# A seven-product matrix multiplication: moving VectorE's second-term sums ahead of a norm's bias passes, and two turned tiles further back on TensorE

## The reference, cut to what matters

```
mix = concat([att, u], -1) @ w_out            # (tokens, 1024) @ (1024, 1024)
h   = layer_norm(ALPHA * h + mix, ln1_g, ln1_b)
v   = mem @ w_cv                              # keys and values of the cross-attention,
q   = h @ w_cq                                # then its queries
```

## Time and profile before

| | us |
|---|---|
| median of three runs | 1035.78 (1035.64 to 1036.3) |
| the profiled execution | 1041.34 |
| its span, first to last instruction | 1039.6 |
| mixer's products of pairs 0 and 1, first to last | 362.21 to 421.51 |

### The profile page before, as it was taken

The page is one execution under the profiler, slowest core; times in us unless marked ns, Lnnn a source line. Parts: engine busy times, 40 slices in busy tenths (PEclk is TensorE's granted clock), DMA queues, the critical chain, the costliest instruction groups (busy, mean ns, idle before and its releaser), DMA issues.

```text
span 1039.6 us, 10109 instructions
## 1 busy us (share of the span) xinstructions
PE 914.8 (88%) x3322; PEld 472.8 (45%) x3322; DVE 524.3 (50%) x830; ACT 237.1 (23%) x582; POOL 321.1 (31%) x352
## 2 busy tenths in 40 slices
PE   4999999799989879999999999967969999999900
PEld 4555466344544434445558544553434444444300
DVE  4899999964632286746225465354311111211156
ACT  5321423234493111201004302131101111111101
POOL 6921043334453252400004403313251221112047
PEclk9999999899999999999999999977989999999955
DMA  9310301403003002220032031356997999998462
GB/s 335 135 41 0 122 0 63 100 1 82 1 1 122 1 0 81 81 82 0 1 116 88 3 160 69 154 240 223 419 404 273 420 421 418 390 416 344 182 245 121
DMA packets 46197, 165.11 MB, mean 159 GB/s; under 512 B 8640, under 2 KB 14144, under 8 KB 33856
## 3 DMA queue, kind: packets, MB, share of 16 engines
q1 hardware_dynamic: 39424, 151.85, 37.9%
q0 software_dynamic: 6720, 12.60, 3.2%
HBM read 156.88 MB, written 18.03 MB: 168 GB/s over the span
## 4 chain that ended last, share of the span: by engine, by line
PE 55%; POOL 4%; DVE 4%; issue 3%; DMA 2%; ACT 1%; POOLq 0%; DVEq 0%
PE ps L2470 8%; PE ps L2499 7%; PE ps L2301 7%; PE ps L2473 5%; PE ps L2340 5%; PE ps L2274 5%; PE ps L2238 4%; PE ps L2006 3%; PE ps L2184 2%; PE ps L2447 2%; PE ps L2109 2%; POOL hres L729 2%; PE ps L2081 1%; PE ps L2330 1%; PE ps L2018 1%
## 5 line engine op out<-in xcount | busy, mean ns | idle before, releaser
L1324 DVE SCALAR_TENSOR_TENSOR cat<-early,cpar,cat 128x798 f32<-128x798 f32 (+2 forms) x150 | 141.6, 944 | 4.9
L844 POOL TENSOR_SCALAR hT<-hT,rinv 128x512 f32<-128x512 f32 (+1 forms) x48 | 67.8, 1424 | 94.1 <-DVE rinv L1446 94.1
L2006 PE MATMUL ps<-ring,hT 128*128 128x512 f32 (+1 forms) x256 | 90.4, 513 | 0.0
L2006 PE MATMUL ps<-hT,ring 128*128 128x256 f32 (+1 forms) x256 | 86.1, 500 | 4.6 <-issue 2.9
L910 POOL DMA_INDIRECT pair_rows<-hT,sidx x22 | 22.1, 1002 | 182.8 <-DVE hT L1933 181.9
L1923 DVE COPY memx<-ps 128x256 f32<-128x256 f32 x22 | 9.3, 424 | 131.2 <-PE ps L2482 131.2
L2006 PEld LDWEIGHTS ps<-hT,ring 128*128 128x128 f32 x256 | 50.5, 199 | 38.8 <-issue 32.9
L718 POOL TENSOR_SCALAR lnt<-mv 128x1 f32<-128x1 f32 x28 | 14.2, 505 | 168.5 <-DVE mv L746 167.4
L2006 PEld LDWEIGHTS ps<-ring,hT 128*128 128x128 f32 x256 | 48.4, 191 | 38.7 <-issue 36.3
L1438 DVE TENSOR_REDUCE nmax<-ps 128x2 f32<-128x1024 f32 (+1 forms) x24 | 25.1, 1046 | 73.5 <-PE ps L2134 73.4
L851 POOL TENSOR_SCALAR memx<-memx,rinv 128x256 f32<-128x256 f32 x24 | 22.0, 924 | 129.7 <-DVE rinv L1402 129.7
(11 more groups left out here) (337 smaller groups left out, 1760.6 us busy)
## 6 DMA issues: line engine op xcount, KB each, us to landing
ring<-w_down SPq DMA_DIRECT2D x16, 1024.0 KB, 17.0
early<-w_gate SPq DMA_DIRECT2D x12, 1024.0 KB, 9.5
early<-w_up SPq DMA_DIRECT2D x12, 1024.0 KB, 13.7
ring<-w_gate SPq DMA_DIRECT2D x10, 1024.0 KB, 12.3
ring<-w_up SPq DMA_DIRECT2D x10, 1024.0 KB, 16.4
scr<-w_down SPq DMA_DIRECT2D x8, 1024.0 KB, 15.6
cat<-w_down SPq DMA_DIRECT2D x8, 1024.0 KB, 15.4
scr<-w_gate SPq DMA_DIRECT2D x5, 1024.0 KB, 9.3
```

Of the source, the lines that this page charges most:

```text
L844: g.tensor_scalar(sprob[u % 4][:, 0:width], sprob[u % 4][:, 0:width], rinv[:, u % 4:u % 4 + 1], None, ALU.mult).then_inc(prob_ready, 1)
L1324: ins = v.scalar_tensor_tensor(out=out, in0=src, scalar=cpar[:, c, k:k + 1], in1=out, op0=ALU.mult, op1=ALU.add)
L2006: last = t.matmul(out_of(bank), lhs(k), rhs(k), start=(k == 0), stop=(k == KC - 1))
```

## The change

Nothing is added or removed; eight pieces change places on two engines. `mix_term(0, "P2")` and `mix_term(1, "P2")` on VectorE stand ahead of the bias pass of tile 0 and of T4, `mix_term(0, "P6")` stands between T4 and T1, the bias pass of tile 0 behind T1, and that of tile 1 behind the sum for P7. On TensorE the turned tile 0 comes behind P5 in place of P7, and the turned tile 1 behind P3 in place of P4.

```diff
             mix_rows(0, 3)
             mix_rows(0, 4)
-            dve_bias(dve, LN_1[0], link)
+            mix_term(0, "P2")
+            mix_term(1, "P2")
             dve.wait_ge(mx_combined, 4)
             v.tensor_tensor(mxT["T4"], mxB[1][0], mxT["T2"], ALU.subtract).then_inc(mx_combined, 1)
+            mix_term(0, "P6")
             v.tensor_tensor(mxT["T1"], mxB[0][1], mxB[0][0], ALU.subtract).then_inc(mx_combined, 1)
+            dve_bias(dve, LN_1[0], link)
+            mix_term(0, "P7")
             dve_bias(dve, LN_1[1], link)
-            mix_term(0, "P2")
-            mix_term(1, "P2")
-            for term in ("P6", "P7", "P4", "P5"):
-                mix_term(0, term)
+            mix_term(0, "P4")
+            mix_term(0, "P5")
...
                 mx_term(a, "P7", mxS["S3"], mxT["T3"])
                 if a == 0:
-                    h1_T(0)
                     pe.wait_ge(mx_combined, 7)
                 mx_term(a, "P4", A22, mxT["T4"])
                 if a == 0:
-                    h1_T(1)
                     pe.wait_ge(mx_combined, 8)
                 mx_term(a, "P5", mxS["S1"], mxT["T1"])
+                if a == 0:
+                    h1_T(0)
                 pe.wait_ge(mx_combined, (6, 12)[a])
                 mx_term(a, "P3", mxS["S4"], mxB[1][1])
+                if a == 0:
+                    h1_T(1)
```

## The result

| | before | changed |
|---|---|---|
| median of the eleven runs of each that were then compared | 1039.80 (1034.91 to 1043.26) | 1031.37 (1028.32 to 1035.36) |
| ratio, 95% interval | | 0.9934 (0.9914 to 0.9953) |
| profiled execution | 1041.34 | 1032.55 |
| its span | 1039.6 | 1030.8 |

Faster, by 8.4 us between the medians; the interval of the ratio is 4.9 to 8.9 us of 1039.8. The profiled execution became 8.79 us shorter, against 8.8 forecast (1032.5); that they agree so closely is in part luck, since the parts that the change does not touch came out alike in these two profiles and differ by some us in others (the last table of the experiments). The median, 1031.37, lies above the range that the prediction gave (1025.8 to 1029.8): the kernel before, run eleven times, has its median 4 us above that of the three runs shown first.

A forecast was written before the change was run, and what follows sets the result against it. TensorE, busy 914.8 of 1039.6 us, was taken as the bound. 9.47 us of wait and slow clock, less new waits of 0.5 and 0.2, gave 8.8; 1035.78 - 8.8 = 1027.0 us, range 1025.8 to 1029.8.

The forecast's parts named there:

- P7's wait: TensorE ahead of P7 of pair 0: 6.45 us of waiting for the bank of P2 would go.
- The slow clock: TensorE during P7 of pair 0: clock at 0.50 of full cost 3.02 us, which would be regained.
- The new wait for ScalarE's copy: VectorE's P2 sum of pair 1 waits for ScalarE, then is held by GpSimd's gain; P4 starts 0.5 us late.
- The wait of 0.2 ahead of P5: TensorE ahead of P5 of pair 0: T1 done at 386.85, P5 starts at 386.95, a wait of 0.2 us.
- Turned tiles: Moved transposes on TensorE: both bias passes in time, by 2.4 and 3.6 us, so the moves cost nothing.
- The long new wait: Rival: L720 stays held whatever VectorE does, P4 3.2 us late; gain 6.0 (1029.7); chance 0.09.
- The gain wasn't absorbed: Rival: a later stage, a load above all, does not move with the products; time stays 1035.8; chance 0.06.
- that last rival: Clock falls at the short waits ahead of P4 and P5, stays down until P6 of pair 1 ends; 1040.8; chance 0.05.
- The step that failed is the last one: Whole time: the shown runs' median, 1035.78, lies 5.56 us below the profiled execution; less 8.8 gives 1027.0.

The follow-up runs named there:

- P6 three times: Kernel before, with P6 of pair 0 computed three times into its bank so TensorE does not stand; stretch from first P1 to first `w_cv` product 58.97 us, one run 1040.73.
- copying first: Whole change plus ScalarE's copy of P1 of pair 1 ahead of its normalising of tile 1; ratio to before 0.9934, stretch 52.09 us.
- the kernel before once more: Kernel before, unedited, profiled and timed again; median 1040.39 us of 12 runs, ratio 1.0009, stretch from first P1 to first `w_cv` product 61.14.
- TensorE's order alone: Kernel before with only the change's TensorE moves, VectorE in the old order; median 1036.78 us, ratio 0.9987, stretch 61.27.

## Why the prediction was right in its mechanism and wrong in its number

**P7's wait: right.** It waited for the bank of P2 of pair 0; with the sum first, P7 follows P6 in one row of 7.03, as P6 and P7 of pair 1 do, and 6.45 of waiting are gone.

**The slow clock: right in its price.** It was priced at 3.02; it is 2.6 to 3.0 over the profiles with P7's wait in full, and goes where TensorE doesn't stand (P6 three times). But the clock was not down "for all of P7", as the prediction says under its rivals; in the trace of before it rose within P7's last 1.3 us:

```profile
391.00:392.30 1.30, 1.30 (x4) 0.48 (x3) 0.00 (x0) 0.00 (x0) 0.00 (x0) 0.70 0.00 0
```

**The new wait for ScalarE's copy: right** (forecast, measured in brackets). L720 done at 375.95 (375.96), copy done at 377.70 (377.72), the L1506 held by the gain to 380.26 (380.28), T4 the last thing that P4 waits for. P4 starts at 383.3 (383.26), 0.5 late (0.51). The wait of 0.2 ahead of P5 did not come as a wait of its matmuls: P5 starts on time, and P4 and P5 lose about 0.1 each at their first weight load. Together the loss was to be 0.7, and copying first gives back 0.73.

**Turned tiles: right.** They didn't wait; their two moves are free given VectorE's order, and needed by it (5.02 of wait without them).

**Rivals.** The long new wait didn't come: L720 is not held beyond the one L1506 (0.80). The gain wasn't absorbed. The clock did not fall at the short waits, in any of three profiles (0.35, 0.34 and 1.40). My argument against that last rival was weaker than it read: it used one stretch at a clock of 1.00, and in the second profile of the same program the clock did fall between 340 and 361:

```profile
340.00:361.00 21.00, 18.24 (x75) 8.91 (x73) 3.98 (x8) 3.51 (x8) 6.19 (x4) 0.92 0.01 1
```

**The step that failed is the last one:** "The median of the runs shown is 5.56 below that execution; I take the same gain off it", with bounds that reached below by "the runs shown spread by 0.66". I took the 5.56 for something that goes with the profiler, and laid the gain on a base, 1035.78, that was too low. That term is what was mis-sized: over the eleven runs of before the median lies 1.54 below the profiled execution and not 5.56, and for the changed kernel 1.18. In six sets of runs (those of the changed kernel and of five experiments) the profiled execution lies from 1.16 below to 4.02 above the median; so there is no fixed 5.56, though a smaller part that goes with the profiler is not excluded. 1039.80 - 8.8 is 1031.0, and 1031.37 was measured. The 63 runs of before that I have go from 1034.91 to 1044.61, in two clumps: 22 lie below 1037.5, one from there to 1038.4, and 40 above; the three shown were all of the lower clump, the profiled execution of the upper one. If each run draws for itself, three of the lower clump come some 4 times in 100; whether runs made together draw alike is not shown. The mean of the 63 is 1039.16, that of 17 runs of the changed kernel 1031.36: 7.8 less, against 8.8 forecast and 8.3 to 8.8 in the stretch itself. The prediction's bounds laid around the profiled execution's 1032.5 (1.2 below, 2.8 above) would have held the result only by a hair, from 1031.3 on.

What varies goes with TensorE's clock. In the 12 runs of the kernel before once more, time and mean granted clock go together with a correlation of -0.95, about 1 us for each 0.001: 1043.84 at 0.946, 1035.87 at 0.954. That is the size that the clock alone would give: 0.001 less over 1040 us is 2 us at 0.50, which lose 1 us if TensorE works through them. One place where it varies is the first expert block, where TensorE often stands and where the same 32 matmuls, behind the same wait, took either time (TensorE in order of time and the stretch of these matmuls, first the kernel before once more, then TensorE's order alone):

```profile
715.25 9.94 PE L2470 MATMUL ps<-early,hT 128*64 128x512 f32 x32 [0.83 <-ACT hT L1230]
```

```profile
715.25:725.10 9.85, 9.85 (x32) 3.15 (x32) 0.00 (x0) 1.10 (x1) 1.01 (x1) 0.71 0.54 223
```

```profile
715.40 7.09 PE L2472 MATMUL ps<-early,hT 128*64 128x512 f32 x32 [0.83 <-ACT hT L1230]
```

```profile
715.40:722.40 7.00, 7.00 (x32) 2.62 (x32) 0.00 (x0) 1.11 (x1) 1.01 (x1) 1.00 0.77 317
```

Why the times of before fall into just two clumps stays open: I have no profile of the lower clump of that very program, so it isn't shown either that its stretch takes 61 us there too.

## What to carry to other kernels

Where a consumer of PSUM banks stands idle, look at what is queued ahead of the read that frees the bank: here a pass that waited on a chain over three engines held a 1.4 us read back by 9 us, and the two halves of the reorder, worth 2.1 to 2.6 us (VectorE's) and nothing clear of the spread (TensorE's) each alone, gave 8.3 to 8.8 together. Two VectorE instructions in a row with two SBUF operands each held up GpSimd's smallest instruction over both (1.85 and 3.46 us), and one with an instruction behind it that reads PSUM over one (0.80); so leave a gap, or an operand in PSUM, where such an instruction is on the path. Predict and check a change on the length of the stretch that it touches, which came again within 0.44 and 0.02 us here, and don't lay the gain on a median of three runs before knowing how far the runs of one program lie apart (here 9.7 us).

## What the runs showed of the hardware that was not expected

TensorE's granted clock was lower behind a wait of 2.86 us (0.69 over the product behind it) and of 5.02 (0.55), where I had left open whether 3 us would do it; behind waits of 1.40 and 0.35 it was not. Up to 387.40 in the wait of 5.02 that ended at 387.48 it was still at 1.00, and over the wait of 6.29 it was at 0.93: it fell late in the wait or only as the work came back, and stayed low over the first part of that work.

P4 and P5 of the changed kernel took 3.54 and 3.53 at full clock (383.26 to 386.80 to 390.33), against 3.43 for both in the version with the copy first (381.82 to 385.25 to 388.68). Weight loads in order of time, the first loads of P4 and of P5 in the changed kernel, then the first load of P4 with the copy first:

```profile
383.26 0.30 PEld L2240 LDWEIGHTS ps<-early,cat 128*128 128x128 f32 x2 [1.18 <-DVE early L1576]
...
386.79 0.30 PEld L2240 LDWEIGHTS ps<-ring,memx 128*128 128x128 f32 x2 [0.66 <-DVE ring L1578]
```

```profile
381.39 0.19 PEld L2240 LDWEIGHTS ps<-early,cat 128*128 128x128 f32 x1 [0.24 <-issue]
```

In the changed kernel the first load of each waits for T4 or T1 and starts with the product's first matmul; with the copy first it runs 0.43 ahead of it (381.39, 381.82). So T1 cost P5 0.1 us, though no wait stands ahead of P5 in TensorE's row.
